# A transformer kernel's first transfers, cut to one tile of x and one slab of weights, and its first products, put ahead of the second turn of x

## The chip, the core and the metric

The kernel runs on one core of a Trainium2 chip. The metric is the device time of one execution in microseconds (us). The core's engines each work through a queue of their own: TensorE (in profiles PE, its weight loads PEld) multiplies and transposes into PSUM banks, VectorE (DVE), ScalarE (ACT) and GpSimd (POOL) do the elementwise work, and SyncE (SP) mostly issues transfers from device memory. Order between engines comes from semaphores that the program sets and waits on by hand.

## The reference, cut to what matters

Two transformer blocks over one sequence of 512 tokens with 1024 features, in float32. What is computed first, and what the change touches, is the value projection of the first block:

```python
h = rmsnorm(x, norm_mix_g[l])            # x * rsqrt(mean(x*x) + eps) * g
proj = jnp.einsum('bsd,dc->bsc', h, w_in[l])
u, v, bg, cg, xs, ga, gb = jnp.split(proj, split_at, axis=-1)
...
v = rmsnorm(jax.nn.gelu(v, approximate=False), norm_v_g[l])
a = spatial_gating(u, v, w_s[l], b_s[l])
```

Behind it come the rest of the first block (gating, a causal convolution, three projections, a feed-forward part) and the second one (modulation, two kinds of attention, a feed-forward part, a last norm).

## The kernel before, in words

Features are split into 8 tiles of 128 (`KT`), tokens into 4 blocks of 128 (`NBLK`). x is loaded with tokens on the partitions (`gates`) and must be turned, so that features lie on the partitions (`x_features`): 4 transposes on TensorE for each tile, one for each token block, into one PSUM bank (`turn_x(c)`, line 950, turns tiles 2c and 2c+1).

Every product is made in three parts, since operands and weights are split into a rounded high part and a rest (`hi`, `lo`): high by high, low by high, high by low. For weights, ScalarE rounds (`weights`, line 1444) and VectorE subtracts (`weights`, line 2023). For x, the bank is copied to `x_features` (tiles 0, 1 and the odd ones by VectorE in `keep_x`, the even ones from 2 on by ScalarE), ScalarE scales by the gain and rounds (`scale_x`), VectorE makes the rest (`split_scaled_x`).

The first stage is the first half of v, `first_values(0, b, kt)`: for each k-tile kt, 4 token blocks by 3 parts, 12 products of 128x512. Its operand is not yet divided by the norm; that division is done where the banks are read. Its weights are 8 slabs of 128x512, of which the first two are split singly (`first_slab`) and the others in pairs. On TensorE the order is written out by hand: filler products that keep the array busy (`keep_array_busy`), turns of x, and products, where the turns of tiles 4 to 7 stand behind the products of k-tiles 0 and 1:

```python
keep_array_busy(4)
turn_x(0)
keep_array_busy(5)
pe.wait_ge(table_kept, 1)
turn_x(1)
...
    for b in range(NBLK):
        first_values(0, b, kt)
    if kt < 2:
        turn_x(kt + 2)
    if kt == 6:
        spread_rms("n1")
```

The products of k-tile kt wait for the operand's tile (`operand`) and for the weights' low part (`first_lo` for slab 0, then `w_lo_done`, which counts slab 1 as one and each later pair as one). On ScalarE the order behind tile 1 is: tiles 2 and 3, weights of slabs 2 and 3, tiles 4 and 5, the squares of one token block, tiles 6 and 7, weights of slabs 4 to 7, the other squares and the norm. VectorE follows it, the reciprocal of the norm last.

SP issues the transfers in program order: x tiles 0 and 1 (`load_x(0)`), weight slabs 0 and 1 (`value_slabs`), x tiles 2 and 3, slabs 2 and 3, the other x tiles, slabs 4 to 7; then it waits for low parts (`w_lo_done`) before it loads the next weights into the same buffers.

Of the kernel before, what the change touches and what calls it, by code (L numbers as in the profile page):

```python
# [15 lines left out]
P = 128  # L16
# [6 lines left out]
NBLK = S // P  # L23
# [187 lines left out]
def build(nc, a, out):  # L211

    ctx = ExitStack()
    with ctx:
        def sb(name, cols, dt=F32, parts=P):
            return ctx.enter_context(nc.sbuf_tensor(name, [parts, cols], dt))

        def sem(name):
            return ctx.enter_context(nc.semaphore(name))
# [37 lines left out]
        gates = sb("gates", KT * S)  # L257
# [95 lines left out]
        def tile(buf, n):  # L353
            return buf[:, bass.ds(n * S, S)]

        def col(c, n=1):
            return table[:, bass.ds(c, n)]

        gain_loaded, vec_loaded, late_loaded, ws_loaded, small_loaded = (
            sem(n) for n in ("gain_loaded", "vec_loaded", "late_loaded", "ws_loaded", "small_loaded"))  # L360
        x_loaded = [sem(f"x_loaded{c}") for c in range(4)]
        consts, masks_begun = sem("consts"), sem("masks_begun")
        rows_turned, table_kept, ws_turned, ws_kept, x_turned, x_kept, act_kept = (
            sem(n) for n in ("rows_turned", "table_kept", "ws_turned", "ws_kept", "x_turned", "x_kept", "act_kept"))
        first_landed, first_hi, first_lo = sem("first_landed"), sem("first_hi"), sem("first_lo")
        c_ready, gain2_done = sem("c_ready"), sem("gain2_done")
        x_sumsq, v_done = sem("x_sumsq"), sem("v_done")
        raw_landed = [sem(f"raw_landed{j}") for j in range(2)]
# [58 lines left out]
        def diagonals(buf, kind):  # L427

            if kind == 0:
                return buf.rearrange("p (e b n) -> p e b n", e=HEADS_AT_ONCE, n=2 * P)[:, :, :, 0:P]  # L430
            return heads(buf, 0, P)

        def x_free(d):

            return (act_kept, d // 2) if d >= 2 and d % 2 == 0 else (x_kept, d + 1 if d < 2 else (d + 3) // 2)
# [40 lines left out]
        def rows(w):  # L476
            return w.rearrange("(k p) n -> p k n", p=P)

        def slab(buf, first, n):

            return buf[:, first * S:(first + n) * S]
# [70 lines left out]
        def _(sp):  # L552
            xt = a["x"][0].rearrange("(b p) n -> p b n", p=P)

            def load_x(c):
                cs = slice(c * 2 * P, (c + 1) * 2 * P)
                sp.dma_start(gates[:, :].rearrange("p (b n) -> p b n", b=NBLK)[:, :, cs], xt[:, :, cs])\
                  .then_inc(x_loaded[c], 16)
# [17 lines left out]
            def value_slabs(q, j, first, n, landed):  # L576

                sp.dma_start(slab(raw[j], first, n).rearrange("p (k n) -> p k n", n=S),
                             rows(w_in)[:, HALF * j + first:HALF * j + first + n, D + S * q:D + S * (q + 1)])\
                  .then_inc(landed, 16)  # L580

            for half, landed in enumerate((first_landed, raw_landed[0])):
                load_x(half)
                value_slabs(0, 0, 2 * half, 2, landed)
            for c in range(2, 4):
                load_x(c)
            value_slabs(0, 1, 0, HALF, raw_landed[1])
# [249 lines left out]
        def _(pe):  # L837
# [99 lines left out]
            def spread_rms(norm, bank=1):  # L937

                pe.wait_ge(inv_done, NORM[norm] + 1)
                for b in range(NBLK):  # L940
                    mm = pe.transpose(aux[bank][:, b * P:(b + 1) * P],
                                      rms[:, NBLK + b:NBLK + b + 1].to_broadcast([P, P]), ident[:, :])
                mm.then_inc(norm_spread, 1)
# [4 lines left out]
            pe.transpose(aux[1][:, 0:KT], vec_rows[0:KT, 0:P], ident[0:KT, 0:KT]).then_inc(rows_turned, 1)  # L948

            def turn_x(c):  # L950
                pe.wait_ge(x_loaded[c], 16)
                for d in (2 * c, 2 * c + 1):
                    if d >= 4:
                        pe.wait_ge(*x_free(d - 4))
                    for b in range(NBLK):
                        mm = pe.transpose(X_BANKS[d % 4][:, b * P:(b + 1) * P],
                                          gates[:, b * D + d * P:b * D + (d + 1) * P], ident[:, :])
                    mm.then_inc(x_turned, 1)
# [5 lines left out]

            keep_array_busy(4)
            turn_x(0)
            keep_array_busy(5)
            pe.wait_ge(table_kept, 1)
            turn_x(1)

            def turn_spatial_weights():
                pe.wait_ge(ws_loaded, 16)
# [5 lines left out]
            def first_values(q, b, kt):  # L978

                wh, wl = (slab(w, kt, 1) for w in (w_hi_all, w_lo_all))  # L980
                ah, al = (op[:, kt * S + b * P:kt * S + (b + 1) * P] for op in OP[1])
                pe.matmul(ps[b][:, :], ah, wh, start=(kt == 0), stop=False)  # L982
                pe.matmul(ps[b][:, :], al, wh, start=False, stop=False)  # L983
                mm = pe.matmul(ps[b][:, :], ah, wl, start=False, stop=(kt == KT - 1))  # L984
                if b == 3 and kt % 2 == 1:

                    mm.then_inc(tile_done, 1)
                elif b < 3 and kt == KT - 1:
                    mm.then_inc(v_done, 1)
# [15 lines left out]
            for kt in range(KT):  # L1005
                if kt == 0:
                    pe.wait_ge(first_lo, 1)
                else:
                    pe.wait_ge(w_lo_done, kt // 2 + 1)
                pe.wait_ge(operand, MADE["x0"] + kt + 1)  # L1010
                for b in range(NBLK):
                    first_values(0, b, kt)
                if kt < 2:
                    turn_x(kt + 2)
                if kt == 6:
                    spread_rms("n1")
            pe.wait_ge(vec_loaded, 6 * 16)
# [186 lines left out]
            for event in MIXER:  # L1204
                kind, n = event
# [237 lines left out]
        def _(act):  # L1443
# [75 lines left out]
            def scale_x(d):  # L1519

                act.wait_ge(*x_free(d))
                act.activation(tile(hi1, d), tile(x, d), ACT.Copy, scale=col(C_NMIX + d)).then_inc(act_hi, 1)

            def first_slab(kt, signal):
                act.activation(slab(w_hi[0], kt, 1), slab(raw[0], kt, 1), ACT.Copy).then_inc(signal, 1)

            def square_by_token(b):
                if b > 0:
                    act.wait_ge(x_sumsq, b)
                else:  # L1530
                    for c in range(4):
                        act.wait_ge(x_loaded[c], 16)
                act.activation(tB[:, :], gates[:, b * D:(b + 1) * D], ACT.Square,
                               accum_out=stat[:, b:b + 1]).then_inc(x_sumsq, 1)

            act.wait_ge(first_landed, 16)
            first_slab(0, first_hi)
            scale_x(0)
            first_slab(1, w_hi_done)
            scale_x(1)  # L1540
            for d in range(2, KT):
                if d % 2 == 0:
                    act.wait_ge(x_turned, d + 1)
                    act.activation(tile(x, d), X_BANKS[d % 4][:, :], ACT.Copy).then_inc(act_kept, 1)
                scale_x(d)
                if d == 3:
                    act.wait_ge(raw_landed[0], 16)
                    weights(0, 1)
                if d == 5:
                    square_by_token(0)  # L1550
            for k in (2, 3):
                weights(0, k)
            for b in range(1, NBLK):
                square_by_token(b)
# [247 lines left out]
            for event in MIXER:  # L1802
                kind, n = event
                if kind == "part":
                    if n[2] < KT:
                        continue
                    kind, n = "tile", n[0]
# [32 lines left out]
                elif kind == "fg" and n > 0:  # L1840
                    p = n - 1
# [4 lines left out]
                elif kind == "decayed":  # L1846
                    p = n
# [174 lines left out]
        def _(dve):  # L2022
# [72 lines left out]
            def keep_x(d):  # L2095
                dve.wait_ge(x_turned, d + 1)
                dve.tensor_copy(tile(x, d), X_BANKS[d % 4][:, :]).then_inc(x_kept, 1)

            def split_scaled_x(d):
                dve.wait_ge(act_hi, MADE["x0"] + d + 1)  # L2100
                dve.scalar_tensor_tensor(out=tile(lo1, d), in0=tile(x, d), scalar=col(C_NMIX + d),
                                         in1=tile(hi1, d).bitcast(F32), op0=ALU.mult, op1=ALU.subtract).then_inc(operand, 1)

            def first_slab(kt, ready, signal):
                dve.wait_ge(ready, 1)
                dve.tensor_tensor(slab(w_lo[0], kt, 1), slab(raw[0], kt, 1), slab(w_hi[0], kt, 1).bitcast(F32),
                                  ALU.subtract).then_inc(signal, 1)

            for d in range(2):
                keep_x(d)  # L2110
            first_slab(0, first_hi, first_lo)
            split_scaled_x(0)
            first_slab(1, w_hi_done, w_lo_done)
            split_scaled_x(1)
            for d in range(2, KT):
# [390 lines left out]
            for event in VECTOR_MIXER:  # L2506
                kind, n = event
                if kind == "part":
                    if n[2] < KT:
                        continue  # L2510
                    kind, n = "tile", n[0]
# [78 lines left out]
                elif kind == "sp":  # L2590
# [6 lines left out]
                    d = diagonals(E[n % 3], which)  # L2597
# [242 lines left out]
```

## Time and profile before

| | |
|---|---|
| median of 3 runs | 1409.53 us (1409.06 to 1410.84) |
| profiled execution, its own time | 1409.77 us |
| its span, first to last instruction | 1408.1 us |
| TensorE busy | 1392.1 us (99%) |
| VectorE busy | 903.8 us (64%) |
| ScalarE busy | 606.4 us (43%) |
| GpSimd busy | 118.0 us (8%) |

The profile is of one execution, and its times count from the start of the span. Busy time of TensorE is modelled, since its matmuls are pipelined. The chain that ended last is followed back from the last instruction, at each step to what released it. "Windows" give busy time, granted TensorE clock (1.00 is full) and traffic for a stretch of time.

### The profile page before, as it was taken

The numbers are of one execution on the slowest core, as the hardware profiler recorded it, in microseconds if no ns is written. First come the engines' busy times: TensorE is split into PE (matmuls) and PEld (weight loads), VectorE is DVE, ScalarE is ACT, GpSimd is POOL, SyncE is SP. The second block draws the span as 40 slices with busy tenths as digits, with TensorE's granted clock in tenths as the row PEclk, the third lists the DMA queues.
The fourth block names the chain that finished last, engine by engine and source line by source line (L and its number), as shares of the span: only waits on it lengthen the run. The fifth ranks groups of instructions, "written<-read, shape, count | busy, mean of one in ns | idle before, by whom it ended". The sixth has DMA issues, their size and how long they took to land.

```text
span 1408.1 us, 17288 instructions
## 1 busy us (share of the span) xinstructions
PE 1392.1 (99%) x6585; PEld 1148.8 (82%) x6585; DVE 903.8 (64%) x1243; ACT 606.4 (43%) x822; POOL 118.0 (8%) x135
## 2 busy tenths in 40 slices
PE   9999999999999899999999999999999999999998
PEld 8888888888888788888888877777799888888887
DVE  5555644677378664774855666667668664777693
ACT  6543322223224453543533445547545453544432
POOL 1000000000000213021000000000012002001120
PEclk9999999999999999999999999999999999999999
DMA  7244455446545798869452313030158729624621
GB/s 243 93 135 135 136 178 166 148 135 209 190 140 196 250 228 240 209 200 234 134 187 86 119 44 106 3 118 31 60 150 250 198 81 269 188 90 113 201 76 60
DMA packets 140418, 212.22 MB, mean 151 GB/s; under 512 B 3873, under 2 KB 104335, under 8 KB 139583
## 3 DMA queue, kind: packets, MB, share of 16 engines
q1 hardware_dynamic: 112992, 127.67, 28.0%
q0 software_dynamic: 26736, 83.21, 22.0%
q8 instruction: 43, 0.70, 0.2%
q10 hardware_dynamic: 623, 0.43, 0.1%
q14 instruction: 24, 0.20, 0.0%
HBM read 198.58 MB, written 7.48 MB: 146 GB/s over the span
## 4 chain that ended last, share of the span: by engine, by line
PE 83%; DVE 9%; ACT 3%; issue 2%; DMA 2%; DVEq 0%; ACTq 0%; POOL 0%; SPq 0%; POOLq 0%
PE bank L860 17%; PE bank L862 17%; PE bank L861 17%; PE aux L1080 14%; PE bank L1185 5%; DMA raw<-in_w_up 2%; DVE weights_lo L2037 2%; PE aux L1421 1%; PE bank L1421 1%; DVE ada_sums L2216 1%; PE bank L984 1%; PE bank L982 1%; PE bank L983 1%; ACT weights_hi L1467 1%; PE bank L1317 1%
## 5 line engine op out<-in xcount | busy, mean ns | idle before, releaser
L860 PE MATMUL bank<-operand_hi,weights_hi 128*128 128x512 f32 x1248 | 488.8, 392 | 1.1 <-DVE weights_lo L2037 0.8
L862 PE MATMUL bank<-operand_hi,weights_lo 128*128 128x512 f32 x1248 | 486.5, 390 | 0.0
L861 PE MATMUL bank<-operand_lo,weights_hi 128*128 128x512 f32 x1248 | 486.4, 390 | 0.0
L2037 DVE TENSOR_TENSOR weights_lo<-raw,weights_hi 128x1024 fp32r<-128x1024 f32 (+1 forms) x190 | 235.5, 1247 | 165.8 <-ACT weights_hi L1467 164.1
L860 PEld LDWEIGHTS bank<-operand_hi,weights_hi 128*128 128x128 f32 x1248 | 234.8, 188 | 51.2 <-DVE weights_lo L2037 1.8
L862 PEld LDWEIGHTS bank<-operand_hi,weights_lo 128*128 128x128 f32 x1248 | 234.7, 188 | 49.0
L861 PEld LDWEIGHTS bank<-operand_lo,weights_hi 128*128 128x128 f32 x1248 | 234.7, 188 | 48.1
L1467 ACT ACTIVATE weights_hi<-raw 128x1024 fp32r<-128x1024 f32 (+1 forms) x190 | 197.7, 1047 | 167.0 <-PE bank L862 65.2
L2216 DVE SCALAR_TENSOR_TENSOR ada_sums<-ada_or_attention,c_silu,ada_sums 128x384 f32<-128x384 f32 x112 | 69.2, 618 | 3.4
L1472 ACT ACTIVATE operand_hi<-value 128x512 fp32r<-128x512 f32 (+1 forms) x40 | 25.3, 633 | 99.6 <-DVE value L2271 39.0
L1951 ACT ACTIVATE conv_or_gate<-bank,vector_table 128x512 f32<-128x512 f32 x44 | 34.0, 773 | 68.1 <-PE bank L862 66.6
L1080 PE MATMUL aux<-weights_hi,operand_hi 128*128 128x512 f32 x160 | 62.2, 389 | 0.0
L1080 PE MATMUL aux<-weights_hi,operand_lo 128*128 128x512 f32 x160 | 62.2, 389 | 0.0
L1080 PE MATMUL aux<-weights_lo,operand_hi 128*128 128x512 f32 x160 | 62.2, 389 | 0.0
L2730 DVE SCALAR_TENSOR_TENSOR conv_or_gate<-bank,vector_table,conv_or_gate 128x511 f32<-128x511 f32 x44 | 32.9, 747 | 45.2 <-ACT conv_or_gate L1951 45.0
L2345 DVE TENSOR_TENSOR gates<-gates,aux 128x512 f32<-128x512 f32 x54 | 35.4, 685 | 27.3 <-PE aux L1080 27.3
L2389 DVE SCALAR_TENSOR_TENSOR evacuated<-bank,inverse_rms_diagonals 128x512 f32<-128x512 f32 x32 | 22.0, 686 | 44.6 <-PE bank L862 26.5
L701 POOL DMA_DIRECT2D ada_or_attention<-in_w_ada x16 | 14.2, 887 | 413.0 <-DVE ada_sums L2216 350.5
L1080 PE MATMUL aux<-weights_hi,down_weights_hi 128*128 128x512 f32 x120 | 46.7, 389 | 0.0
L1080 PE MATMUL aux<-weights_hi,scores_low 128*128 128x512 f32 x120 | 46.7, 389 | 0.0
L1080 PE MATMUL aux<-weights_lo,down_weights_hi 128*128 128x512 f32 x120 | 46.7, 389 | 0.0
L1185 PE MATMUL bank<-operand_hi,weights_hi 128*128 128x512 f32 x112 | 44.2, 394 | 0.0
(404 smaller groups left out, 2075.9 us busy)
## 6 DMA issues: line engine op xcount, KB each, us to landing
raw<-in_w_in SPq DMA_DIRECT2D x39, 1024.0 KB, 5.3
raw<-in_w_ff SPq DMA_DIRECT2D x29, 1024.0 KB, 6.4
ada_or_attention<-in_w_ada POOLq DMA_DIRECT2D x16, 1536.0 KB, 7.9
raw<-in_w_up SPq DMA_DIRECT2D x22, 1024.0 KB, 6.6
x_features<-in_w_ff POOLq DMA_DIRECT2D x12, 1024.0 KB, 11.0
raw<-in_w_out SPq DMA_DIRECT2D x8, 1024.0 KB, 4.9
x_features<-in_w_down POOLq DMA_DIRECT2D x8, 1024.0 KB, 11.0
raw<-in_w_down SPq DMA_DIRECT2D x6, 1024.0 KB, 5.0
```

The source lines that it names most:

```text
L860: pe.matmul(dst[:, :], wh, ah, start=(kt == 0), stop=False)
L861: pe.matmul(dst[:, :], wh, al, start=False, stop=False)
L862: mm = pe.matmul(dst[:, :], wl, ah, start=False, stop=(kt == k_tiles - 1))
L1080: mm = pe.matmul(banks_of[b][:, :], lhs, rhs, start=(m in (0, 1, 3) and kt == 0 and n == 0), stop=(kt == PAIRS - 1 and n == 2), skip_group ...
L1185: mm = pe.matmul(dst, stationary, moving, start=(kt == 0 and n == 0), stop=(kt == KT - 1 and n == 2))
L1421: mm = pe.matmul(dst, lhs, rhs, start=False, stop=(kt == LAST_K - 1), skip_group_check=True)
L1467: act.activation(slot[:, 0:k_tiles * P].rearrange("p (k n) -> p k n", n=P), src[:, :, k % 2 * P:(k % 2 + 1) * P], ACT.Copy).then_inc(w_hi_ ...
L1951: act.activation(yb[:, k * S:(k + 1) * S], ps[k][:, :], ACT.Identity, bias=col(C_BCONV + ct), scale=col(C_WCONV + 2 * F2T + ct)).then_inc( ...
L2037: dve.tensor_tensor(lo[:, 0:k_tiles * P].rearrange("p (k n) -> p k n", n=P), src[:, :, k % 2 * P:(k % 2 + 1) * P], hi[:, 0:k_tiles * P].bi ...
L2216: dve.scalar_tensor_tensor(out=sums, in0=src, scalar=cvec[:, kt:kt + 1], in1=sums, op0=ALU.mult, op1=ALU.add).then_inc(ada_step, 1)
L2345: dve.tensor_tensor(y, y, banks_of[b][:, :], op).then_inc(read, 1)
L2730: dve.scalar_tensor_tensor(out=y[:, 1:S], in0=ps[k][:, 0:S - 1], scalar=col(C_WCONV + F2T + ct), in1=y[:, 1:S], op0=ALU.mult, op1=ALU.add) ...
```

## The change

SP loads x tile 0 and weight slab 0, then x tile 1 and slab 1, each as a transfer of its own; before, tiles 0 and 1 and slabs 0 and 1 came as pairs. Two new semaphores, `x_first_loaded` and `second_landed`, tell tile 0 and slab 1. TensorE waits for tile 1 only between the transposes of tile 0 and those of tile 1. `turn_x(1)` moves from ahead of the products to behind those of k-tile 0, and the turns of tiles 4 to 7 move back by one k-tile too. VectorE copies x tile 1 only after it has split slab 0 and x tile 0.

```diff
-            for half, landed in enumerate((first_landed, raw_landed[0])):
-                load_x(half)
-                value_slabs(0, 0, 2 * half, 2, landed)
+            def load_x_tile(d, landed):
+                ds = slice(d * P, (d + 1) * P)
+                sp.dma_start(gates[:, :].rearrange("p (b n) -> p b n", b=NBLK)[:, :, ds], xt[:, :, ds]).then_inc(landed, 16)
+
+            load_x_tile(0, x_first_loaded)
+            value_slabs(0, 0, 0, 1, first_landed)
+            load_x_tile(1, x_loaded[0])
+            value_slabs(0, 0, 1, 1, second_landed)
+            load_x(1)
+            value_slabs(0, 0, 2, 2, raw_landed[0])
...
             def turn_x(c):
-                pe.wait_ge(x_loaded[c], 16)
+                if c == 0:
+                    pe.wait_ge(x_first_loaded, 16)
+                else:
+                    pe.wait_ge(x_loaded[c], 16)
                 for d in (2 * c, 2 * c + 1):
+                    if d == 1:
+                        pe.wait_ge(x_loaded[0], 16)
...
             keep_array_busy(5)
             pe.wait_ge(table_kept, 1)
-            turn_x(1)
...
-                if kt < 2:
-                    turn_x(kt + 2)
+                if kt < 3:
+                    turn_x(kt + 1)
...
             first_slab(0, first_hi)
             scale_x(0)
+            act.wait_ge(second_landed, 16)
             first_slab(1, w_hi_done)
...
-            for d in range(2):
-                keep_x(d)
+            keep_x(0)
             first_slab(0, first_hi, first_lo)
             split_scaled_x(0)
+            keep_x(1)
             first_slab(1, w_hi_done, w_lo_done)
```

TensorE's queue from the second fillers on, before (`L963` are fillers, `L956` transposes of x, `L982` to `L984` the three parts of a product):

```order
L963 MATMUL aux<-identity,ones 128x128 x5
L956 MATMUL aux<-identity,gates 128x128 [waits x_loaded1,table_kept]
L956 MATMUL aux<-identity,gates 128x128 x7
L982 MATMUL bank<-weights_hi,operand_hi 128x512 [waits operand,first_lo]
...
L956 MATMUL aux<-identity,gates 128x128 [waits x_kept,x_loaded2]
...
L982 MATMUL bank<-weights_hi,operand_hi 128x512 [waits operand,w_lo_done]
```

And the same place with the change (`L976` are fillers, `L969` transposes, `L994` the first part of a product):

```order
L976 MATMUL aux<-identity,ones 128x128 x5
L994 MATMUL bank<-weights_hi,operand_hi 128x512 [waits operand,first_lo,table_kept]
...
L969 MATMUL aux<-identity,gates 128x128 [waits x_loaded1]
L969 MATMUL aux<-identity,gates 128x128 x7
L994 MATMUL bank<-weights_hi,operand_hi 128x512 [waits operand,w_lo_done]
...
L969 MATMUL aux<-identity,gates 128x128 [waits x_kept,x_loaded2]
```

The turn of tiles 2 and 3 has moved behind the 12 products of k-tile 0, that of tiles 4 and 5 behind k-tile 1.

VectorE's queue from its first copy of x on, before (`L2097` copies x, `L2106` makes the low part of a slab, `L2101` the rest of x, `L2028` the low part of two slabs):

```order
L2097 COPY x_features<-aux 128x512 [waits x_turned,table_kept]
L2097 COPY x_features<-aux 128x512 [waits x_turned]
L2106 TENSOR_TENSOR weights_lo<-raw,weights_hi 128x512 [waits first_hi]
L2101 SCALAR_TENSOR_TENSOR operand_lo<-x_features,vector_table,operand_hi 128x512 [waits act_hi]
L2106 TENSOR_TENSOR weights_lo<-raw,weights_hi 128x512 [waits w_hi_done]
...
L2101 SCALAR_TENSOR_TENSOR operand_lo<-x_features,vector_table,operand_hi 128x512 [waits act_hi] x2
L2028 TENSOR_TENSOR weights_lo<-raw,weights_hi 128x1024 [waits w_hi_done]
```

And with the change (`L2111`, `L2120`, `L2115` and `L2042` are the same four):

```order
L2111 COPY x_features<-aux 128x512 [waits x_turned,table_kept]
L2120 TENSOR_TENSOR weights_lo<-raw,weights_hi 128x512 [waits first_hi]
L2115 SCALAR_TENSOR_TENSOR operand_lo<-x_features,vector_table,operand_hi 128x512 [waits act_hi]
L2111 COPY x_features<-aux 128x512 [waits x_turned]
L2120 TENSOR_TENSOR weights_lo<-raw,weights_hi 128x512 [waits w_hi_done]
...
L2115 SCALAR_TENSOR_TENSOR operand_lo<-x_features,vector_table,operand_hi 128x512 [waits act_hi] x2
L2042 TENSOR_TENSOR weights_lo<-raw,weights_hi 128x1024 [waits w_hi_done]
```

The copy of x tile 1 has moved behind the rest of tile 0; from there on the order is the same.

## Rows read from the trace of the kernel before

**Rows 1.** Page, part 1: busy us (share of the span) and instructions.
```profile
PE 1392.1 (99%) x6585; PEld 1148.8 (82%) x6585; DVE 903.8 (64%) x1243; ACT 606.4 (43%) x822; POOL 118.0 (8%) x135
```

**Rows 2.** TensorE's waits: line, waited for, us in total, times, longest.
```profile
PE aux L914 <- DVE square_sums L2060: 3.5, 1, 3.5
...
PE aux L1165 <- DVE mix_bias L2574: 0.9, 1, 0.9
```

**Rows 3.** Chain that ended last, 0 to 130: start us, us, what.
```profile
3.16 2.00 PE aux L963 x8
5.17 1.71 PE aux L956 x8
6.87 2.13 PE aux L963 x10
9.01 0.87 PE aux L956 x8
9.88 0.23 PE bank L982
...
12.62 0.87 PE aux L956 x8
...
16.25 0.87 PE aux L956 x8
17.12 0.23 PE bank L982
```

**Rows 4.** Timeline, SP's issues: start us, us, queue, line, out<-in, count.
```profile
0.94 0.44 SPq L557 DMA_DIRECT2D gates<-in_x  x1
...
1.44 0.49 SPq L578 DMA_DIRECT2D raw<-in_w_in  x1
...
1.98 0.47 SPq L557 DMA_DIRECT2D gates<-in_x  x1
```

**Rows 5.** DMA issues (the three of group 4; 22.06 us): KB each, us to landing.
```profile
gates<-in_x SPq DMA_DIRECT2D x1, 512.0 KB, 3.5
...
raw<-in_w_in SPq DMA_DIRECT2D x1, 512.0 KB, 4.7
...
gates<-in_x SPq DMA_DIRECT2D x1, 512.0 KB, 6.2
...
raw<-in_w_in SPq DMA_DIRECT2D x1, 1024.0 KB, 5.5
```

**Rows 6.** Timeline, VectorE and ScalarE, 6 to 24.6: start us, us, engine, line.
```profile
6.13 1.47 DVE L2097 COPY x_features<-aux 128x512 f32<-128x512 f32 x2 [2.77 <-PE aux L956]
...
7.52 0.68 DVE L2106 TENSOR_TENSOR weights_lo<-raw,weights_hi 128x512 fp32r<-128x512 f32 x1
...
8.12 0.75 DVE L2101 SCALAR_TENSOR_TENSOR operand_lo<-x_features,vector_table,operand_hi 128x512 fp32r<-128x512 f32 x1
...
9.48 0.60 ACT L1544 ACTIVATE x_features<-aux 128x512 f32<-128x512 f32 x1 [0.77 <-PE aux L956]
...
11.39 1.05 ACT L1453 ACTIVATE weights_hi<-raw 128x1024 fp32r<-128x1024 f32 x1
...
12.47 1.22 DVE L2028 TENSOR_TENSOR weights_lo<-raw,weights_hi 128x1024 fp32r<-128x1024 f32 x1 [0.19 <-ACT weights_hi L1453]
...
19.67 2.36 DVE L2028 TENSOR_TENSOR weights_lo<-raw,weights_hi 128x1024 fp32r<-128x1024 f32 x2
...
24.35 0.18 DVE L2124 RECIPROCAL rms_by_token<-rms_by_token 128x4 f32<-128x4 f32 x1 [2.32 <-ACT rms_by_token L1556]
```

**Rows 7.** Chain that ended last, 464 to 482, behind the 3.5 us wait.
```profile
471.15 0.43 PE bank L861
...
473.25 0.23 PE bank L860
```

**Rows 8.** Windows: us, busy by engine, PEclk, DMA share, GB/s.
```profile
470.00:480.00 10.00, 10.00 (x41) 8.03 (x40) 2.18 (x4) 2.96 (x5) 2.73 (x4) 0.85 0.97 314
990.00:1000.00 10.00, 9.08 (x55) 7.03 (x54) 6.51 (x11) 6.76 (x10) 0.41 (x1) 1.00 0.00 0
```

More of the change, by code:

```diff
@@ L361, in build @@
         x_loaded = [sem(f"x_loaded{c}") for c in range(4)]
+        x_first_loaded, second_landed = sem("x_first_loaded"), sem("second_landed")
         consts, masks_begun = sem("consts"), sem("masks_begun")
@@ L1530, in square_by_token @@
                 else:
+                    act.wait_ge(x_first_loaded, 16)
                     for c in range(4):
```

## The prediction

> **What bounds the kernel now.** I read the page's busy times first. TensorE's matmuls fill 1392.1 of 1408.1 us [rows 1], and the list of who waited for whom gives TensorE one long wait past the start, 3.5 us behind a sum of squares; another, taken here for its size, is 0.9 us [rows 2]. Neither lies where the change is. Busy time alone proves little for pipelined matmuls, so the chain that ended last comes next, in its first 18 us [rows 3]. The reader is to see that the chain there is TensorE alone, each piece starting where the one before ends: 4 filler products to 5.17 us, 8 transposes of x (tiles 0 and 1) to 6.87, 5 fillers to 9.01, 8 transposes (tiles 2 and 3) to 9.88, then the 12 products of k-tile 0 to 12.62. TensorE waits for no transfer here, and not for the operands of the first product either: their last part, the split of x tile 0 on VectorE, runs from 8.12 for 0.75 us and is there at 8.87 [rows 6], before the transposes end at 9.88.
>
> The chain also shows how fast the array goes. The first 8 transposes take 1.71 us and the second 8 take 0.87 [rows 3]. By this spacing the first stretch is at the lower of the two levels (1.2 GHz), and the array reaches 2.4 GHz at about 9.0 us, just as the second fillers end and after some 6 us of unbroken work. The change leaves all fillers in.
>
> Then the transfers. SP issues x tiles 0 and 1, weight slabs 0 and 1, and x tiles 2 and 3 at 0.94, 1.44 and 1.98 us [rows 4], and they land 3.5, 4.7 and 6.2 us after their issue [rows 5], thus at 4.44, 6.14 and 8.18. The first is wanted by TensorE at 5.17, the third at 9.01. Both have time to spare.
>
> **The change, part by part.**
>
> *Smaller first transfers.* Two issues of 512 KB become four of 256 KB, two more issues of about 0.5 us each on SP [rows 4]. SP's queue then runs about 1 us later, but it holds transfers that land one behind the other anyway: 1.70 us (6.14 − 4.44) and 2.04 us (8.18 − 6.14) for 512 KB. x tile 0 and weight slab 0 come earlier, at 4.44 or before and at about 4.44 to 5.3. Worth: nothing, since TensorE is in its fillers until 5.17 as before, and the transposes of tile 0 end at 5.17 + 4 × 0.214 = 6.03.
>
> x tile 1 is now third in the queue, and TensorE wants it at 6.03. How long a transfer of one tile takes is not in the trace. Lower bound: half of a 512 KB one, 0.85 us, so that it lands at 4.44 + 0.85 = 5.3. Upper bound: it has as many runs as two tiles, each half as long; if time goes by runs, it takes the 2.04 us of a two-tile one behind 0.85 us of weights, and lands at 7.3. I take the lower, the nearer row being the bytes' rate, which is much the same for the long runs of weights and the short ones of x. The upper end costs a wait of 1.3 us.
>
> Here the Trainium skill speaks against the change: "DMA: Bandwidth & Descriptors", section "Rules for kernel authors", wants 1 MiB or more per transfer for full bandwidth, and its section "Anatomy of one DMA — SWDGE (gpsimd) path" gives each transfer a fixed cost of about 2.0 us. The trace does not show such a cost once per transfer: the second 512 KB land 1.70 us behind the first. If it were paid in series all the same, an estimate from the page's figures, 3 × 2.6 us after 0.94, would bring x tile 1 at 8.7 and add 2.7 us to the sum.
>
> *First products ahead of the next turn.* TensorE does the same instructions in another order: 12 products and 8 transposes change places. Moving 0.87 us of transposes behind 2.74 us of products (9.88 to 12.62 [rows 3]) saves nothing on an engine that is never idle. It pays only if the first product is ready at 9.01 and no later one becomes late.
>
> It is ready. VectorE copies x tile 0 from 6.13 for 1.47 / 2 = 0.74 us, makes the low part of slab 0 in 0.68, and splits x in 0.75 [rows 6]: 8.30, or 0.7 us before 9.01. The copy of tile 1, which came in between before, now follows. Products of k-tile 0 run from 9.01 to 11.75, tiles 2 and 3 are turned to 12.62, k-tile 1 runs to 15.36. Its split comes after a copy (0.74), a low part (0.68) and a split (0.75), at about 10.5.
>
> *What is late next.* Tiles 2 and 3 are now turned at 11.75 instead of 9.01, tiles 4 and 5 and tiles 6 and 7 likewise one k-tile later. Behind each turn in the queues of ScalarE and VectorE stand not only the x tiles but weight pieces, in an order that is unchanged. Two matter.
>
> First, weights of k-tiles 2 and 3. Before: tile 2 is turned at 9.01 + 0.44 = 9.45, ScalarE starts at 9.48, rounds the weights from 11.39, and VectorE has the low part at 12.47 + 1.22 = 13.69 [rows 6]. That is 4.24 us after the turn, with almost no idle time in it, and the products began at 17.12 [rows 3], 3.4 us later. Now: tile 2 turned at 11.75 + 0.44 = 12.19, weights at 16.43. TensorE arrives at 15.36 + 0.87 = 16.23. A wait of 0.2 us.
>
> Second, weights of k-tiles 4 and 5, which both engines do only after x tiles 6 and 7. Before: tile 6 turned at 16.25 + 0.44 = 16.69, the low part done at 19.67 + 1.22 = 20.89 [rows 6], 4.20 us later; the products of k-tile 4 began at 17.12 + 2 × 2.74 = 22.6, 1.7 us of room. Now: k-tile 2 runs 16.43 to 19.17, tile 6 is turned at 19.61, the weights are there at 23.81. TensorE arrives at 19.17 + 0.87 + 2.74 = 22.78. A wait of 1.0 us.
>
> Bounds of the two: from nothing (if the engines run ahead of these lags) to 1.6 us, if 0.2 us for waking and refilling comes to each. I take the lags as measured: 1.2 us. The remaining weights, of k-tiles 6 and 7, are one pass of 1.22 us behind (25.0) and wanted at 23.81 + 2 × 2.74 = 29.3. The inverse norm, next on both engines, moves by 2.9 us from 24.5 [rows 6] to 27.4 and is wanted after k-tile 6, at 23.81 + 3 × 2.74 = 32.0. SP's next two weight loads wait for these low parts and start 2.7 and 2.9 us later; the later one, which landed 5.5 us after its issue [rows 5], would be there at 25.0 + 5.5 = 30.5, still ahead of that norm, behind which ScalarE takes it.
>
> Sum: 0 (transfers) + 0 (exchange) + 0.2 + 1.0 = +1.2 us. The chain starts on TensorE, so nothing behind gives it back. Profiled execution: 1409.77 + 1.2 = 1410.97. The median of the three runs lies 0.24 us below that execution, so **1410.7 us**, +0.09%. A measurement of this kernel can tell about 0.2%, or 2.8 us, from no change; this is within it.
>
> **The rivals.**
>
> *A. The engines keep up; unchanged, 1409.5 (−0.3 to +0.5).* For it: after a turn the two engines take work in turns, and some of it might go ahead sooner than before. Against: both lags are back-to-back work on two engines, and the second would have to shrink by 1.0 us.
>
> *B. x tile 1 is late by up to 1.3 us, 1411.4 to 1412.0.* The pause falls into the slow stretch. If the array still speeds up at 9.0, half of it is won back in the fillers. For it: the tile's runs are half as long. Against: the room of 0.7 us at 6.03.
>
> *C. Slower: the array reaches its full clock later.* That same pause, or the exchange, could move the moment from 9.01 past the first products. The trace has such a case: after the 3.5 us wait, products go 0.43 us apart up to 473.25 and 0.23 after it [rows 7], and the granted clock of 470 to 480 is 0.85; the 0.9 us wait leaves 990 to 1000 at 1.00 [rows 8]. Twelve products of k-tile 0 at 0.43 instead of 0.23 cost 2.4 us; with the 1.2 that is 1413.1. It decides if x tile 1 comes well after 6.03 and the fillers after it start the warming anew. The waits of 0.2 and 1.0 us later are of the size that left the clock up.
>
> *D. Transfers pay in series.* If each took the first one's 3.5 us, x tile 1 would land at 0.94 + 3 × 3.5 = 11.4, 5.4 us after 6.03: 1409.5 + 1.2 + 5.4 = 1416.1. The landings 1.70 and 2.04 us apart speak against it. It is the Trainium skill's fixed cost paid in series, as above.
>
> *E. Faster: the clock comes up before the fillers end.* Then TensorE would reach the second turn early, wait for x tiles 2 and 3 until 8.18 and start products at 8.18 + 0.87 = 9.05, where the changed kernel could start at 8.30: −0.75 us, 1408.8 if the two waits stay away too. Against it: nothing in the traced execution waits there.
>
> **How the numbers follow.** Forecast 0.62, A 0.13, B 0.12, E 0.04, C 0.07, D 0.02. All but C and D lie within 2.8 us of 1409.5. So slower by over 0.2% is 0.09. Of E I count half, 0.02, as faster by over 0.2%, for a start gained beyond the 0.75 us that the rows show; the rest, 0.89, is the same. The range takes in A, the forecast's bounds and B: 1409.0 to 1412.3, leaving out C, D and E.
>
> **What would show it.** In the profile after: the first transposes start near 5.0 as before and x tile 1 causes no gap at 6.0; product of k-tile 0 starts near 9.0 with 0.23 us spacing; TensorE waits for the low part of weights twice, about 0.2 us near 16.4 and 1.0 us near 23.8. Wrong would be no such waits (A), a gap before the fifth transpose (B), or products 0.43 us apart after 9.0 (C).

## The result, and the profile after

| | before | after |
|---|---|---|
| median | 1409.82 us (11 runs, 1409.06 to 1410.84) | 1413.83 us (11 runs, 1411.08 to 1414.27) |
| profiled execution | 1409.77 us | 1411.27 us |
| its span | 1408.1 us | 1409.7 us |
| TensorE busy | 1392.1 us | 1392.2 us |

The changed kernel is slower: ratio 1.0022, 95% interval 1.0014 to 1.0031; the medians alone lie 4.0 us apart. The changed kernel's executions fall in two groups, three from 1411.1 to 1411.6 and seven from 1413.3 to 1414.3, with one between them, and the profile is of a short one. So the trace explains 1.5 us directly, and the rest took experiments.

The chain that ended last in the kernel after, in its first 25 us (start us, us, what; `L976` are fillers, `L969` transposes of x, `L994` and `L995` parts of products, beside [rows 3]):

```profile
3.17 2.01 PE aux L976 x8
5.17 1.97 PE aux L969 x8
7.14 1.28 PE aux L976 x10
8.52 0.47 PE bank L994
8.99 0.23 PE bank L995
...
11.49 0.45 PE aux L969 x4
...
16.19 0.50 PE bank L994
16.70 0.24 PE bank L995
...
19.25 0.45 PE aux L969 x4
...
23.96 0.50 PE bank L994
24.46 0.23 PE bank L995
```

The first product starts at 8.52 instead of 9.88. The first product of k-tile 4 starts at 23.96 and has its 0.50 us; before, it stood at 17.12 + 2 × 2.74 = 22.60 with 0.23. That is 23.96 + 0.27 − 22.60 = 1.6 us lost, against 1.5 between the two profiled executions. From the first product on, the kernel lost 15.71 − 12.72 = 3.0 us: 0.87 for the second turn, which now stands inside, 1.3 for waits, and three times about 0.25 for a first product that starts on an empty array (0.47, 0.50, 0.50 instead of 0.23). The earlier start gave 1.36 of it back. Part of that start is the clock's: the fillers behind x take 1.28 us here, 2.13 in [rows 3], so the array was at its full clock at about 7.2 us, not at 9.0.

The waits, from the list of who waited for whom on TensorE after (us in total, times, longest); the same list of the kernel before has no wait of these products (`L982` there):

```profile
PE bank L994 <- DVE weights_lo L2042: 1.3, 2, 1.1
```

The start, from the timeline of TensorE's weight loads after (start us, us, then idle before and what ended it):

```profile
4.75 0.87 PEld L969 LDWEIGHTS aux<-identity,gates 128*128 128x128 f32 x4
6.03 0.71 PEld L969 LDWEIGHTS aux<-identity,gates 128*128 128x128 f32 x4 [0.40 <-DMA gates<-in_x]
```

Here TensorE pauses for x tile 1. The transfers behind that, from the timeline of SP's issues (start us, us) and the DMA issues of those stretches (KB each, us from issue to landing), beside [rows 4, 5]:

```profile
0.94 0.44 SPq L585 DMA_DIRECT2D gates<-in_x  x1
1.44 0.49 SPq L579 DMA_DIRECT2D raw<-in_w_in  x1
1.98 0.44 SPq L585 DMA_DIRECT2D gates<-in_x  x1
2.46 0.50 SPq L579 DMA_DIRECT2D raw<-in_w_in  x1
```

```profile
gates<-in_x SPq DMA_DIRECT2D x1, 256.0 KB, 2.7
...
raw<-in_w_in SPq DMA_DIRECT2D x1, 256.0 KB, 3.9
...
gates<-in_x SPq DMA_DIRECT2D x1, 256.0 KB, 4.0
...
raw<-in_w_in SPq DMA_DIRECT2D x1, 256.0 KB, 5.0
```

Landings: 3.64, 5.34, 5.98 and 7.46. The first tile is 0.8 us sooner than the pair was, but the same 1 MB is there at 7.46 instead of 6.14, and tile 1 lands at 5.98 instead of the 5.3 of the forecast. In the other traces with this order of transfers tile 1 lands between 5.6 and 7.2 (3.6 to 5.2 us after its issue at 1.98).

### The profile page after: what moved, and what is told of

It reads as the page before. It is cut to its first block, busy times and chain, and to the rows that moved or that the text cites. A ratio compares the mean times of both kernels' runs of the same rounds, so it can differ in the third digit from the quotient of the medians.

```text
span 1409.7 us, 17289 instructions
## 1 busy us (share of the span) xinstructions
PE 1392.2 (99%) x6585; PEld 1147.7 (81%) x6585; DVE 902.4 (64%) x1243; ACT 606.6 (43%) x822; POOL 118.2 (8%) x135
## 4 chain that ended last, share of the span: by engine, by line
PE 83%; DVE 9%; ACT 3%; issue 2%; DMA 2%; DVEq 0%; ACTq 0%; POOL 0%; SPq 0%; POOLq 0%
PE bank L868 17%; PE bank L870 17%; PE bank L869 17%; PE aux L1092 14%; PE bank L1197 5%; DMA raw<-in_w_up 2%; DVE weights_lo L2051 2%; PE aux L1433 1%; PE bank L1433 1%; DVE ada_sums L2230 1%; PE bank L994 1%; PE bank L995 1%; PE bank L996 1%; ACT weights_hi L1479 1%; PE bank L1329 1%
```

## The experiments

Theory 1: the pause for x tile 1 makes the array's full clock late in part of the executions. Theory 2: the waits for weights are all there is, by their time or by a clock that falls in them. Theory 3: something late in the program. For the late tile, and for again_d and again_e, theory 2 is that only the time of the pause counts, at full speed. "Clock" below is the mean granted clock that each execution reports. It does not show a late start: from 5 to 10 us it reads 1.00 in every trace of this study, also where the spacing of transposes and fillers is that of the lower level. When the full clock comes is read from the spacing.

**More traces of the changed kernel, no edit** (again_a, again_b; later again_d, again_e).

> The changed kernel as it is, one more look. Its executions spread from 1411.1 to 1414.3 us, and the profile that is at hand is one of the short ones. Theory 1 (late clock): an execution near 1414 has products of k-tile 0 or k-tile 1 that go 0.43 us apart, at the lower level, by some 12 of them, and the same two waits for weights (0.2 and 1.1 us). Theory 2 (the waits let the clock fall): the first products are 0.23 us apart, and products behind the wait near 24 us are 0.43 apart for some 3 us. Theory 3 (something late in the program): the first 40 us are as in the profile at hand, and the time is lost at one of the later waits.

> The changed kernel as it is, a second look for the same question as in the look before it. Theory 1: near 1414 us the first products are 0.43 us apart; near 1411 us they are 0.23 apart from 8.5 us on. Theory 2: the slow products stand behind the wait near 24 us. Theory 3: both looks agree in the first 40 us whatever their time.

Measured: 1411.34 and 1411.48 us. Both have the waits of 1.3 us and a first product at 8.52 and 8.54. In the first, TensorE's timeline shows the pause at 0.95 us:

```profile
6.98 0.66 PE L969 MATMUL aux<-identity,gates 128*128 128x128 f32 x4 [0.95 <-DMA gates<-in_x]
7.47 1.28 PE L976 MATMUL aux<-identity,ones 128*128 128x128 f32 x10
8.52 0.47 PE L994 MATMUL bank<-weights_hi,operand_hi 128*128 128x512 f32 x1
```

The fillers take 1.28 us in all, beside 2.34 in the same view of the kernel before: a pause does not always make the clock late, and as long as it comes in time the fillers absorb the late tile. They end about when the operand is there, whose last part VectorE makes from 7.62 for 0.75 us. Neither was a long execution, so neither told the theories apart.

> The changed kernel once more, a look for the trace of an execution near 1414 us. Theory 1: if it takes over 1413 with a granted clock of 0.999 its first products go at the lower level. Theory 2: its first product begins later by the difference, behind a later x tile 1, and is at full speed.

> The same look once more: theory 1, first products at the lower level if it takes over 1413; theory 2, a later first product at full speed.

Measured: 1411.20 and 1412.87. In the first, transposes and fillers are nearly all at full speed, and the first product waits for its operand:

```profile
4.97 1.68 PE L969 MATMUL aux<-identity,gates 128*128 128x128 f32 x8
6.49 1.28 PE L976 MATMUL aux<-identity,ones 128*128 128x128 f32 x10
8.52 0.47 PE L994 MATMUL bank<-weights_hi,operand_hi 128*128 128x512 f32 x1 [0.76 <-DVE operand_lo L2115]
```

The second has fillers of 2.26 us and the first product at 9.02, at full speed, and more time lost far from the change, behind the 3.5 us wait of [rows 2] (last section). No trace caught an execution over 1413, so for the changed kernel itself the long group has none.

**TensorE's order alone** (turn_only).

```diff
# against the kernel before
             pe.wait_ge(table_kept, 1)
-            turn_x(1)
...
-                if kt < 2:
-                    turn_x(kt + 2)
+                if kt < 3:
+                    turn_x(kt + 1)
```

> The kernel before with TensorE's new order alone: transfers stay in pairs, so TensorE has no pause between the transposes of x tile 0 and 1. The two waits for weights (0.2 and 1.0 us) should be there. Theory 1 (the pause behind the small transfer makes the clock late): 1410.6 to 1412.3 us with a spread like that of the kernel before, under 2 us. Theory 2 (the waits let the clock fall): median near 1414. Theory 3: unclear, 1411 to 1414.

Measured: 1412.39 (1411.8 to 1413.35), ratio 1.0019 (1.0010 to 1.0028). Its profile has the waits for weights, 1.3 us, and one for the operand:

```profile
PE bank L981 <- DVE weights_lo L2027: 1.3, 2, 1.1
PE bank L981 <- DVE operand_lo L2100: 0.6, 1, 0.6
```

The moved turn alone makes the kernel slower by 2.7 us of median, just over the end of theory 1's range (1412.3) and less than the whole. Its trace accounts for 2.1 of it: the first product of k-tile 4 starts at 24.42 with 0.50 us. No execution is over 1413.35, and the five over 1413 report a clock of 0.996 or 0.997, the others 0.998 or 0.999. Where they lost it was not traced.

**The transfers, with TensorE's order as before** (transfers_only; VectorE's new order stays in).

```diff
# against the changed kernel
             pe.wait_ge(table_kept, 1)
+            turn_x(1)
...
-                if kt < 3:
-                    turn_x(kt + 1)
+                if kt < 2:
+                    turn_x(kt + 2)
```

> The changed kernel with the second turn of x ahead of the first products again, as before: the four small transfers and their pause of some 0.3 us at 6.0 are there, the two waits for weights are gone. Theory 1: 1409.8 to 1413, a wide spread, median some 2 us above the kernel before. Theory 2: 1409.5 to 1410.5, as before. Theory 3 (transfer times shift later loads): 1411 to 1413 with a first 40 us like that of the kernel before.

Measured: 1410.36 (1408.83 to 1411.86) beside 1409.65 before, ratio 1.0004 (0.9995 to 1.0013). In its trace tile 1 came 1.15 us late and tiles 2 and 3 another 0.22. The small transfers bring no gain and at most a small loss; in the median the 2 us of theory 1 are not seen here. Four of its 11 executions take 1411.1 to 1411.9 at clocks of 0.998 and more, one of them 1.000, where the kernel before, timed beside them, has none over 1411.04, so some of them may hold it; none of the four was traced.

**Fillers ahead of x tile 1, weights sooner, and both**, with the changed kernel as control (again_c).

```diff
# fillers ahead of tile 1 (fill_between)
                     if d == 1:
+                        keep_array_busy(5)
                         pe.wait_ge(x_loaded[0], 16)
...
             turn_x(0)
-            keep_array_busy(5)
# weights sooner (weights_sooner), ScalarE; VectorE likewise
             scale_x(1)
+            act.wait_ge(raw_landed[0], 16)
+            weights(0, 1)
...
-                if d == 3:
-                    act.wait_ge(raw_landed[0], 16)
-                    weights(0, 1)
                 if d == 5:
-                    square_by_token(0)
-            for k in (2, 3):
-                weights(0, k)
+                    weights(0, 2)
+            square_by_token(0)
+            weights(0, 3)
```

> The changed kernel as it is, timed against the kernel before on this chip. In three looks its first product began at 8.52 to 8.54 us although x tile 1 landed anywhere from 6.0 to 7.0, and all three took 1411.3 to 1411.5. Theory 1 (a late x tile 1, and behind it a late full clock): a mix of executions at 1411.4 and at 1413 to 1414.5. Theory 2 (the waits for weights alone): 1411.3 to 1412.3 with no second group.

> The changed kernel with the 5 fillers moved from behind the transposes of x tile 1 to ahead of them, so that the array has no pause while tile 1 is on its way (it is wanted at 8.2 or earlier instead of 6.0). The waits for weights stay. Theory 1: first product at 8.5 to 9.1, all executions at 1411.3 to 1412, no group at 1414. Theory 2: the same times as the changed kernel in the same call, within 0.5 us.

> The changed kernel with the weights of slabs 2 and 3 split ahead of x tiles 2 and 3, and those of slabs 4 and 5 ahead of x tiles 6 and 7, on ScalarE and VectorE. The two waits for weights should be gone, and with them 1.3 us of waiting and a refill of some 0.25 us behind each: from the first product to the first of k-tile 4 it should take 12.7 us as before, instead of 15.4. Both theories: 2.7 us less than the changed kernel. Theory 1: 1408.7 where the start is undisturbed, and up to 1411.5 where it is. Theory 2: 1408.7 with the spread of the kernel before.

> Both of these edits together: fillers ahead of x tile 1, and the weights sooner. Theory 1: 1408.6 to 1409.3 in all executions, a narrow spread, and below the kernel before by 0.5 to 1 us. Theory 2: as the kernel with the weights sooner alone. If neither reaches below the kernel before, the time from the first product on is not what it was before the change.

Measured, with 1409.79 for the kernel before, timed beside them:

| | median, us | lowest to highest | ratio to before (95%) |
|---|---|---|---|
| changed kernel (again_c) | 1413.37 | 1409.89 to 1414.17 | 1.0021 (1.0012 to 1.0030) |
| fillers ahead of tile 1 | 1411.45 | 1409.77 to 1413.58 | 1.0010 (1.0001 to 1.0019) |
| weights sooner | 1410.38 | 1407.99 to 1413.28 | 1.0004 (0.9995 to 1.0013) |
| both | 1409.65 | 1407.84 to 1410.84 | 0.9999 (0.9990 to 1.0008) |

Each edit takes off its part, and together they undo the loss. Fillers that cover tile 1's way take 1.9 us off the median, though all that they change is what TensorE does while tile 1 is under way. The two intervals overlap, but one of 11 executions is over 1413 (1413.58) instead of 6 of 11: this speaks against theory 2, and the last experiments add to it. Theory 1 had expected none. With the weights sooner the waits are gone from the list. The expected 12.7 us from the first product to k-tile 4 was a slip: the moved turn of 0.87 us stands inside that stretch now. The chain of the kernel with both edits:

```profile
8.51 0.47 PE bank L994
...
11.52 0.87 PE aux L970 x8
...
15.15 0.87 PE aux L970 x8
...
18.76 0.87 PE aux L970 x8
```

18.76 + 0.87 + 2.74 = 22.37 is k-tile 4, 13.9 us after the first product, and only 0.2 us sooner than the 22.60 before. So an order without waits gains what the start gains (1.36), less the turn (0.87) and a refill: nearly nothing, which fits that "both" equals the kernel before instead of beating it by 0.5 to 1.

**A tile that is always late, and fewer first fillers** (late_tile, both_early).

```diff
# late_tile, against the changed kernel
             value_slabs(0, 0, 0, 1, first_landed)
-            load_x_tile(1, x_loaded[0])
             value_slabs(0, 0, 1, 1, second_landed)
             load_x(1)
+            load_x_tile(1, x_loaded[0])
# both_early, against both
-            keep_array_busy(4)
+            keep_array_busy(2)
```

> The changed kernel with x tile 1 sent fifth instead of third, behind slab 1 and x tiles 2 and 3, so that it lands near 8.5 us and TensorE always pauses some 2.5 us between the transposes of tile 0 and tile 1. Theory 1 (a pause there makes the full clock late): the fillers and the first products in the profile go at the lower level, 0.43 to 0.46 us apart, until past 11 us, and most executions take 1413.5 to 1415. Theory 2 (only the time of the pause counts): first product near 10.5, all products 0.23 apart, 1412.5 to 1413.5.

Measured: 1416.68 (1415.43 to 1416.84), ratio 1.0051 (1.0037 to 1.0065), longer than either theory said. TensorE's timeline:

```profile
9.44 1.11 PE L969 MATMUL aux<-identity,gates 128*128 128x128 f32 x4 [3.40 <-DMA gates<-in_x]
10.34 2.22 PE L976 MATMUL aux<-identity,ones 128*128 128x128 f32 x10
12.32 0.47 PE L994 MATMUL bank<-weights_hi,operand_hi 128*128 128x512 f32 x1
```

Behind a pause of 3.40 us transposes and fillers go at the lower level throughout (2.22 us for the fillers, where a full clock takes 1.28), up to about 12.3; before, the full clock was there at 9.0. The late tile costs its own time, and the fillers behind it cost nearly twice what they cost at the full clock. The products themselves were at full speed, against theory 1's wording.

> The kernel with both edits (fillers ahead of x tile 1, weights sooner) and 2 fillers instead of 4 ahead of x tile 0, which lands at 3.6 and is wanted at 5.2. The fillers are then the bound of the start: first product at 7.6 to 8.0 instead of 8.5. If the full clock comes as early as in the look at the kernel with both edits (near 8): 0.5 to 0.9 us less than that kernel, 1408.8 to 1409.2. If fewer fillers leave the first products at the lower level, 1409.5 to 1411.

Measured: 1408.61 (1407.67 to 1409.98) beside 1409.29 before, ratio 0.9999 (0.9990 to 1.0008). Its first product starts at 7.67, as expected, and the median is 0.7 us lower; by the interval that is no difference. It is the best version of this study, and none beats the kernel before beyond what can be measured.

**What the long group is** (again_f, tiles_first, no_second_fill).

```diff
# tiles_first, against the changed kernel
             load_x_tile(0, x_first_loaded)
+            load_x_tile(1, x_loaded[0])
             value_slabs(0, 0, 0, 1, first_landed)
-            load_x_tile(1, x_loaded[0])
# no_second_fill, against the changed kernel
             turn_x(0)
-            keep_array_busy(5)
```

> The changed kernel as a control for the two beside it on the same chip: median 1413 to 1414, executions from 1410 to 1414.3 in two groups.

> The changed kernel with x tile 1 sent second, ahead of weight slab 0: it should land by about 5.3 and TensorE should not pause at 6.0; slab 0 lands near 6.0 and is rounded by 6.7, in time for VectorE at 6.8. Fillers stay behind tile 1. Late tile: the group at 1413.5 to 1414.3 is gone, all executions at 1410 to 1412.9 like those with the fillers ahead of tile 1. Something else (that only the place of the fillers changed): the group is still there, median above 1413.

> The changed kernel without the 5 fillers behind x tile 1; it leaves out nothing of the computation. TensorE then idles from the end of tile 1's transposes to the first product at about 8.4. If the late group is a late x tile 1 with fillers pushed behind it, its median falls to 1411 to 1412. If the long group comes from the array's clock, the first products now go at the lower level, 0.43 to 0.46 us apart for 12 or more of them, and the median rises to 1413.5 to 1415.

Measured, with 1410.10 before: the changed kernel as it is 1412.38 (1409.95 to 1414.08; ratio 1.0016, 1.0007 to 1.0025), tiles first 1411.80 (1410.62 to 1413.56; 1.0013, 1.0004 to 1.0022), no second fillers 1413.64 (1411.82 to 1414.10; 1.0022, 1.0013 to 1.0031).

With tile 1 sent second, TensorE does not pause:

```profile
4.96 1.78 PE L969 MATMUL aux<-identity,gates 128*128 128x128 f32 x8
```

One execution of 11 is over 1413, at a clock of 0.997. Of the changed kernel's 33 executions in three series, whose medians lie 4.0, 3.6 and 2.3 us above the kernel before, 17 are over 1413. Of these 12 report a clock of 0.998 or more, no less than the short profiled one, so within its rounding they did not lose more in what the clock record shows, which has the stretch behind the 3.5 us wait in it but not the start. With the pause covered by fillers or with tile 1 sent sooner it is 2 of 22. So the long group goes with a late tile 1, not merely with fillers in a certain place.

Without the second fillers two groups appear in plain sight: 1411.8 to 1412.1 and 1413.6 to 1414.1, all at 0.998 or 0.999. The profile happened to be one of the long ones. Its timeline:

```profile
7.05 1.12 PE L969 MATMUL aux<-identity,gates 128*128 128x128 f32 x4 [0.78 <-DMA gates<-in_x]
8.77 0.77 PE L993 MATMUL bank<-weights_hi,operand_hi 128*128 128x512 f32 x1 [0.60 <-DVE operand_lo L2114]
9.33 0.63 PE L994 MATMUL bank<-weights_hi,operand_lo 128*128 128x512 f32 x1
9.76 0.63 PE L995 MATMUL bank<-weights_lo,operand_hi 128*128 128x512 f32 x1
...
12.51 0.40 PE L993 MATMUL bank<-weights_hi,operand_hi 128*128 128x512 f32 x1
12.75 0.39 PE L994 MATMUL bank<-weights_hi,operand_lo 128*128 128x512 f32 x1
```

After a pause of 0.78 us and another of 0.60 for the operand, products start 0.43 us apart and go on so up to 12; then they are 0.24 apart. Seven products, not the 12 that were expected, at 0.2 us more are 1.4 us, and the first one, 0.56 ahead of the second, adds 0.25. Another 0.25 us is not of this kind: the first filler of this execution starts at 3.34 instead of 3.09, behind a transfer of the norm's gain. Here a late clock is seen at work, in a kernel one edit from the changed one, at the same times as the long group; which of the two pauses made it late, this run does not tell.

When the array reaches its full clock differs between executions in any case: by the spacing, between about 6.0 (again_d) and 9.5 us (weights_sooner) in all other traces of this study but two, with no pause or with one of up to 1.15 us. It comes at about 12 in late_tile and in this one. An estimate from these rows for the changed kernel with tile 1 at 6.5 to 7.0 and the full clock at 12: four transposes (0.90) and ten fillers (1.98), as in late_tile, put the first product at 9.4 to 9.9, and five or six products cost 0.2 more each, 2.1 to 2.4 us in all, where some 2.5 part the two groups. That the long group is this late clock is inferred from that size, from this trace and from the two edits that nearly remove it; it was not caught in a trace of the changed kernel.

## Why the prediction was wrong

Right were the list of what would be late next and both waits: 0.2 and 1.0 us were forecast, 1.3 in two, the longer 1.1, were found, each behind the weights named. Right too was that the earlier landing of tile 0 and slab 0 brings nothing (transfers_only is no faster), and that the exchange by itself saves nothing: both edits together return to the time of the kernel before.

Three terms failed.

*Waking and refilling* was put at nothing, with a bound of 0.2 us for each wait that no row stood behind. It is 0.25 us for a first product that starts on an empty array, and there are three of them. With the waits at 1.3 and the turn at 0.87 that is the 3.0 us above; the start gave back 1.36, of which the forecast had 0.87. So in the profiled execution the sum was 1.5, not 1.2: a size, not the mechanism. That the two lie so close is partly luck. The other 0.49 of the start is the condition of rival E, which got 0.04: the clock came up before the fillers ended, and the first product started at 8.52 where E said 8.30. E's gain went into the turn, the waits and the refills. In again_e the clock came as late as before, and the first product started at 9.02, as forecast.

*x tile 1 lands at 5.3, the lower bound.* It landed at 5.98 in the profile and between 5.6 and 7.2 in other traces. The bytes' rate was not a safe row. Four transfers brought the first megabyte 1.3 us later than two did. The Trainium skill's rule in "DMA: Bandwidth & Descriptors", section "Rules for kernel authors", that full bandwidth wants large transfers, was set aside for the landings of the kernel before; the trace after agrees with it (7.46 against 6.14). The last of the four was also issued 1.0 us later than the last of the two (2.46 against 1.44), and no run parts the two. Rival D, transfers in series, is not what happened: tile 1 landed 0.64 us behind slab 0 in the profile, and in no trace with this order of transfers later than 7.2, against 11.4. The fixed cost that the Trainium skill gives in "DMA: Bandwidth & Descriptors", section "Anatomy of one DMA — SWDGE (gpsimd) path", for transfers issued by GpSimd, was not paid in series by these, which SP issues: the estimate from it was 8.7.

*The pause for tile 1 was put at nothing, and rival C got 0.07.* C had nearly the size (1413.1; measured 1413.8), the condition, a tile 1 well after 6.03, and, as far as is known, the mechanism. The waits for weights did not make the clock fall: behind those of 0.22 and 1.09 us products go 0.23 to 0.24 apart. The pause ahead of the fillers takes the other 2.5 us of the median, in part of the executions; that it does so by a late clock is inferred. Against it I set the room of 0.7 us, which was built on the lower bound just named. The two errors are one: with the upper bound taken for tile 1, a pause of up to 1.3 us in the stretch where the array was still at the lower level was the likely case, not a rival (the longest traced with this order of transfers is 1.15). The Trainium skill says in "TensorE: Matmul & The Clock Gate", section "Part 1: The HAM clock gate", that the number of slow matmuls at the start varies from run to run; the traces here agree, with fillers of one kernel between 1.28 and 2.26 us.

The range ended at 1412.3, short of 1413.83, since it left C out.

## What to carry to other kernels

Where one engine is never idle, moving work on it gains only if something else is waited for; so price what the moved work fed, link by link, and add a refill for every wait that appears (0.25 us here). A pair of transfers cut in four came sooner in its first piece here, by 0.8 us, and later in its last, by 1.3: ask who wants the last piece. A new pause ahead of the full clock cost more here than its own time in part of the executions; fillers ahead of the thing that was waited for, instead of behind it, took most of that away.

## What the runs showed that was not expected

How long the array stays slow after the 3.5 us wait of [rows 2] differs between executions of the same kernel. The granted clock (third value from the end) from 460 to 470 and 470 to 480 us, in the kernel after, and from 470 to 480 in two more traces of it, again_f and again_e:

```profile
460.00:470.00 10.00, 7.04 (x32) 5.48 (x30) 9.03 (x14) 4.45 (x6) 1.09 (x2) 1.00 0.31 112
470.00:480.00 10.00, 9.43 (x39) 7.71 (x40) 1.75 (x4) 1.72 (x4) 2.74 (x4) 0.83 1.01 324
```

```profile
470.00:480.00 10.00, 9.41 (x46) 7.85 (x47) 3.01 (x5) 3.28 (x6) 2.74 (x4) 1.00 1.01 329
```

```profile
470.00:480.00 10.00, 8.88 (x32) 7.27 (x33) 1.94 (x4) 1.81 (x3) 2.74 (x4) 0.66 1.01 336
```

Nothing, 1.7 us and 3.4 us of full-speed time are lost there (10 us times what lacks to 1.00), and the three took 1409.95, 1411.27 and 1412.87 us. From 480 to 490 all three are at 1.00 again. In these three the loss behind this wait, far from the change, differs by more than the 1.3 us that the change's own waits cost. The kernel before and the other versions spread too (0.85 in the same stretch [rows 8], mean clocks from 0.996 to 1.000 in their executions). So much of theory 3 holds.
